# A mixer's attention and recurrence, re-ordered beside a weight stream: rotation next to its projection, ten heads in one staggered sequence, a recurrence without reciprocal

## What is computed

```python
h = rmsnorm(x, g_mix)
q_a, k_a, v_a, x_l, gate_l, q_m, gates = split(h @ w_in)
# local attention: 6 heads of 128, 2 key heads, window of 128 with a sink
q_a, k_a = partial_rope(q_a, positions), partial_rope(k_a, positions)
attn_out = windowed_gqa(q_a, k_a, v_a, attn_sink)
# recurrence in both directions over 768 channels (6 blocks of 128)
xc = centred_depthwise_conv(x_l, conv_w, conv_b)
r, i = sigmoid(xc @ w_r + b_r), sigmoid(xc @ w_i + b_i)
log_a = -8 * r * softplus(-lam)
a = exp(log_a)
bx = sqrt(-expm1(2 * log_a)) * (i * xc)          # then h[t] = a[t] h[t-1] + bx[t]
lru_out = (h_fwd + h_bwd) * gelu(gate_l)
# memory attention: 4 heads over 256 memory rows
mem_out = memory_cross_attention(q_m, k_m, v_m)
g = sigmoid(gates + gate_b)
merged = g0 * (attn_out @ p_attn) + g1 * (lru_out @ p_lru) + g2 * (mem_out @ p_mem)
x = x + merged @ w_out
```

## Time and profile before

| | |
|---|---|
| time, median of 3 runs | 2182.87 us (2181.86 to 2184.75) |
| the profiled execution | 2183.73 us, of which the span takes 2182.0 us |
| the mixer in it | 0 to about 313 us; the part that the change touches, 84 to 240 us |
| PE busy | 2142.5 us, 98% of the span |
| DVE, ACT, POOL busy | 1346.6, 1229.6, 972.0 us |
| granted clock of PE, mean | 0.997 |

### The profile page before, as it was taken

The page is one execution under the profiler, slowest core; times in us unless marked ns, Lnnn a source line. Parts: engine busy times, 40 slices in busy tenths (PEclk is TensorE's granted clock), DMA queues, the critical chain, the costliest instruction groups (busy, mean ns, idle before and its releaser), DMA issues.

```text
span 2182.0 us, 38682 instructions
## 1 busy us (share of the span) xinstructions
PE 2142.5 (98%) x15128; PEld 2009.6 (92%) x15128; DVE 1346.6 (62%) x2631; ACT 1229.6 (56%) x2198; POOL 972.0 (45%) x791
## 2 busy tenths in 40 slices
PE   8999999999999999999999999999999999999999
PEld 7998889999999998888888899899998999899997
DVE  4457652998667756666665865356664864546664
ACT  6567555456777755555555465645445465655443
POOL 5775546999666640000004786560002876561000
PEclk9999999999999999999999999999999999999999
DMA  6443555666444456666665554455665545455665
GB/s 230 153 127 125 161 187 170 187 180 184 143 146 141 144 171 202 193 193 193 193 194 165 184 155 146 136 176 172 184 196 173 176 145 160 133 164 169 186 191 160
DMA packets 102951, 370.16 MB, mean 170 GB/s; under 512 B 11370, under 2 KB 12786, under 8 KB 102132
## 3 DMA queue, kind: packets, MB, share of 16 engines
q1 hardware_dynamic: 102772, 367.69, 54.9%
HBM read 365.53 MB, written 2.11 MB: 168 GB/s over the span
## 4 chain that ended last, share of the span: by engine, by line
PE 85%; DVE 7%; ACT 5%; issue 1%; POOL 1%; DMA 1%; SPq 0%; ACTq 0%; DVEq 0%; POOLq 0%
PE stream_bank L557 16%; PE stream_bank L559 15%; PE stream_bank L558 15%; PE side_bank L557 11%; PE side_bank L558 11%; PE side_bank L559 11%; PE side_bank L856 1%; ACT unit_hi L1124 1%; PE side_bank L855 1%; PE side_bank L635 1%; DVE swa_var L2313 1%; POOL unit_lo L2450 1%; DVE t L1858 1%; PE side_bank L682 1%; ACT squares L1151 1%
## 5 line engine op out<-in xcount | busy, mean ns | idle before, releaser
L2450 POOL TENSOR_TENSOR unit_lo<-raw,unit_hi 128x512 fp32r<-128x512 f32 (+1 forms) x724 | 932.7, 1315 | 404.3 <-ACT unit_hi L1124 403.0
L1124 ACT ACTIVATE unit_hi<-raw 128x1024 fp32r<-128x1024 f32 (+1 forms) x678 | 708.7, 1045 | 195.2 <-PE side_bank L559 73.4
L1676 DVE TENSOR_TENSOR unit_lo<-raw,unit_hi 128x1024 fp32r<-128x1024 f32 (+1 forms) x316 | 389.5, 1233 | 243.1 <-ACT unit_hi L1124 242.5
L557 PE MATMUL stream_bank<-hT_hi,unit_hi 128*128 128x256 f32 x1360 | 400.8, 295 | 4.4 <-POOL unit_lo L2450 4.4
L559 PE MATMUL stream_bank<-hT_hi,unit_lo 128*128 128x256 f32 x1360 | 386.5, 284 | 0.0
L558 PE MATMUL stream_bank<-hT_lo,unit_hi 128*128 128x256 f32 x1360 | 386.4, 284 | 0.0
L557 PE MATMUL stream_bank<-h2T_hi,unit_hi 128*128 128x256 f32 x1152 | 329.6, 286 | 0.0
L559 PE MATMUL stream_bank<-h2T_hi,unit_lo 128*128 128x256 f32 x1152 | 326.0, 283 | 0.0
L558 PE MATMUL stream_bank<-h2T_lo,unit_hi 128*128 128x256 f32 x1152 | 325.8, 283 | 0.0
L557 PEld LDWEIGHTS stream_bank<-hT_hi,unit_hi 128*128 128x128 f32 x1360 | 262.1, 193 | 11.6 <-POOL unit_lo L2450 5.6
L2525 POOL TENSOR_TENSOR gmlp_ws<-gmlp_ws,layer_consts 128x128 f32<-128x128 f32 x8 | 3.4, 461 | 586.5 <-DMA gmlp_ws<-in_gmlp_ws_dram 586.5
(11 more groups left out here) (360 smaller groups left out, 4520.0 us busy)
## 6 DMA issues: line engine op xcount, KB each, us to landing
raw<-in_peer_u_dram SPq DMA_DIRECT2D x128, 512.0 KB, 3.6
raw<-in_peer_v_dram SPq DMA_DIRECT2D x128, 512.0 KB, 3.6
raw<-in_gate_dram SPq DMA_DIRECT2D x64, 512.0 KB, 3.6
raw<-in_gt_dram SPq DMA_DIRECT2D x44, 512.0 KB, 4.2
raw<-in_up_dram SPq DMA_DIRECT2D x44, 512.0 KB, 4.1
raw<-in_ffn_out_dram SPq DMA_DIRECT2D x44, 512.0 KB, 4.2
raw<-in_branch_dram SPq DMA_DIRECT2D x32, 512.0 KB, 3.6
raw<-in_w_gate_dram SPq DMA_DIRECT2D x24, 512.0 KB, 3.6
```

Source lines behind the costliest of these rows:

```text
L557: mm(out, l.hi, r.hi, start=start, stop=False)
L1124: activation(k.unit_hi[n % SPLIT_SLOTS][:, 0:w], k.raw[n % RAW_SLOTS][:, 0:w], ACT.Copy).then_inc(k.sem("unit_hi"), 1)
L1676: V.tensor_tensor(k.unit_lo[s][:, 0:w], k.raw[n % RAW_SLOTS][:, 0:w], k.unit_hi[s][:, 0:w], ALU.subtract).then_inc(unit_lo, 1)
L2450: last = G.tensor_tensor(k.unit_lo[s][:, cols], k.raw[n % RAW_SLOTS][:, cols], k.unit_hi[s][:, cols], ALU.subtract)
```

## The change

`staggered` is `pipeline` with a list of start rounds. The rotation leaves `attention()` and becomes a side generator of its own that starts with unit qk 0, in the order 0 to 7; its matmul goes to side bank `SIDE + 4`, which the recurrence's gates use too, so that these wait for the mark "rope". DVE's product with the sine goes to a scratch tile in SBUF, which frees the bank at once. Memory and local heads form one sequence with the start rounds `HEAD_STARTS`, counted from the round of qm 3. In the recurrence DVE now forms a*a and (a*a + 1) * b, with -0.25 in place of -0.5 under the root. The weights of the recurrence come in six pieces between stream loads. The rest of the diff is semaphore counts for the new order.

```diff
+def staggered(generators, starts):
+    live, rounds = [], 0
+    waiting = list(zip(starts, generators))
+    while waiting or live:
+        while waiting and waiting[0][0] <= rounds:
+            live.append(waiting.pop(0)[1])
...
-ROPE_ORDER = (6, 7, 0, 1, 2, 3, 4, 5)
+HEAD_STARTS = (0, 2, 4, 6, 9, 12, 15, 18, 21, 24)
...
 (PE, lru; the same on ACT and DVE)
+            while "rope" not in at.stages:
+                yield
             for half in range(LRU_BLOCKS // LRU_BATCH):
...
 (PE)
         def rope():
-            for c in ROPE_ORDER:
+            for c in range(8):
                 while not at.reached("qk", c):
                     yield
-                bank = take(SIDE + 2 + ROPE_ORDER.index(c) % 2, ("rope", c))
+                bank = take(SIDE + 4, ("rope", c))
                 pe.wait_ge(*k.over["qk", c])
-                if c == ROPE_ORDER[0]:
+                if c == 0:
                     pe.wait_ge(k.sem("landed_mix_consts"), 16)
+                    pe.wait_ge(k.sem("lru_conv"), LRU_BLOCKS)
                 mm(bank[:, 0:TOKENS], k.swap1, k.qk[:, c, :], start=True, stop=True).then_inc(k.sem("rope_mm"), 1)
                 yield
+            at.stages.add("rope")
             yield
...
-            at.stages.add("p_mem")
-            yield from rope()
-            yield from pipeline([head(Head(k, "attn", h), [k.over["rope", h], k.over["rope", 6 + h // 3], k.over["va", 1]])
-                                 for h in range(Q_HEADS)])
+            attn = [head(Head(k, "attn", h), [(k.sem("rope_done"), 7 + h // 3), k.over["va", 1]]) for h in range(Q_HEADS)]
+            mem[-1] = at.finished("p_mem", mem[-1])
+            yield from staggered(mem + attn, HEAD_STARTS)
             at.stages.add("p_attn")
...
-        at.run(main(), [token_norm(), lru(), attention()])
+        at.run(main(), [token_norm(), lru(), rope(), attention()])
...
 (ACT)
-                activation(b_[:, :, :, :], b_[:, :, :, :], ACT.Sqrt, scale=-0.5).then_inc(k.sem("lru_roots"), 1)
+                activation(b_[:, :, :, :], b_[:, :, :, :], ACT.Sqrt, scale=-0.25).then_inc(k.sem("lru_roots"), 1)
...
 (DVE)
-            own.then(V.tensor_scalar(t1[:, :, :], b_[:, j, :, :], -1.0, 1.0, ALU.mult, ALU.add))
-            own.then(V.reciprocal(t1[:, :, :], t1[:, :, :]))
-            V.tensor_tensor(b_[:, j, :, :], b_[:, j, :, :], t1[:, :, :], ALU.mult)
+            own.then(V.tensor_tensor(t1[:, :, :], a_[:, j, :, :], a_[:, j, :, :], ALU.mult))
+            V.scalar_tensor_tensor(b_[:, j, :, :], t1[:, :, :], 1.0, b_[:, j, :, :], ALU.add, ALU.mult)
...
+                if c >= 2:
+                    dve.wait_ge(k.sem("rope_done"), c - 1)
+                dve.wait_ge(k.sem("rope_mm"), c + 1)
+                V.tensor_tensor(swapped(c), k.bank[SIDE + 4][:, 0:TOKENS], k.rope_s[:, :], ALU.mult).then_inc(
+                    k.free[SIDE + 4], 1)
+                if c:
+                    add(c - 1)
+                yield
...
 (SP)
-    load_until(U["va", 0])
-    fetch(k.lru_w[:, :, :], a["lru_w"].rearrange("p (a e) -> p a e", a=24), "landed_lru_w")
+    for i in range(6):
+        load_until(U["va", 0] + i)
+        fetch(k.lru_w[:, 4 * i:4 * i + 4, :], lru_w[:, 4 * i:4 * i + 4, :], "landed_lru_w")
```

More of the change, by code:

```diff
@@ L249, in pipeline @@
         yield
+def staggered(generators, starts):
+    live, rounds = [], 0
+    waiting = list(zip(starts, generators))
+    assert len(starts) == len(generators)
+    while waiting or live:
+        while waiting and waiting[0][0] <= rounds:
+            live.append(waiting.pop(0)[1])
+        for x in list(live):
+            if next(x, "end") == "end":
+                live.remove(x)
+        rounds += 1
+        yield
 class Own:
@@ L769, in attention @@
                 yield
-            yield from pipeline([head(Head(k, "mem", h), [k.over["qm", h], k.over["km", h], k.over["vm", 1]])
-                                 for h in range(MEM_HEADS)])
-            at.stages.add("p_mem")
-            yield from rope()
-            yield from pipeline([head(Head(k, "attn", h), [k.over["rope", h], k.over["rope", 6 + h // 3], k.over["va", 1]])
-                                 for h in range(Q_HEADS)])
+            mem = [head(Head(k, "mem", h), [k.over["qm", h], k.over["km", h], k.over["vm", 1]]) for h in range(MEM_HEADS)]
+            attn = [head(Head(k, "attn", h), [(k.sem("rope_done"), 7 + h // 3), k.over["va", 1]]) for h in range(Q_HEADS)]
+            mem[-1] = at.finished("p_mem", mem[-1])
+            yield from staggered(mem + attn, HEAD_STARTS)
             at.stages.add("p_attn")
@@ L1298, in attention @@
             act.wait_ge(unit_mm, U["vm", 3] + 1)
-            yield from pipeline([head(Head(k, "mem", h)) for h in range(MEM_HEADS)])
-            at.stages.add("p_mem")
-            yield from rope()
-            yield from pipeline([head(Head(k, "attn", h)) for h in range(Q_HEADS)])
+            mem = [head(Head(k, "mem", h)) for h in range(MEM_HEADS)]
+            mem[-1] = at.finished("p_mem", mem[-1])
+            yield from staggered(mem + [head(Head(k, "attn", h)) for h in range(Q_HEADS)], HEAD_STARTS)
             at.stages.add("p_attn")
@@ L1913, in rope, with add @@
         def rope():
-            turned = lambda i: k.bank[SIDE + 2 + i % 2][:, 0:TOKENS]
-            def add(i):
-                c = ROPE_ORDER[i]
-                dve.wait_ge(k.sem("rope_mul"), i + 1)
-                V.tensor_tensor(k.qk[:, c, :], k.qk[:, c, :], turned(i), ALU.add).then_inc(k.free[SIDE + 2 + i % 2], 1)
-            for i, c in enumerate(ROPE_ORDER):
+            swapped = lambda c: k.squares[:, 0, c % 2 * TOKENS:(c % 2 + 1) * TOKENS]
+            def add(c):
+                dve.wait_ge(k.sem("rope_mul"), c + 1)
+                dve.wait_ge(*k.over["rope", c])
+                V.tensor_tensor(k.qk[:, c, :], k.qk[:, c, :], swapped(c), ALU.add).then_inc(k.sem("rope_done"), 1)
+            for c in range(8):
                 while not at.reached("qk", c):
                     yield
-                if i == 0:
+                if c == 0:
                     dve.wait_ge(k.sem("rope_tables"), 1)
-                dve.wait_ge(k.sem("rope_mm"), i + 1)
-                own.then(V.tensor_tensor(turned(i), turned(i), k.rope_s[:, :], ALU.mult))
-                if i:
-                    add(i - 1)
+                if c >= 2:
[5 more added lines that the diff above has]
+                    add(c - 1)
                 yield
-            add(len(ROPE_ORDER) - 1)
+            add(7)
+            at.stages.add("rope")
             yield
@@ L2474, in rope @@
         def rope():
-            yield from steps(4)
-            while not at.reached("qm", MEM_HEADS - 1):
-                yield
-            yield from pipeline([steps(6) for h in range(MEM_HEADS)])
-            for i, c in enumerate(ROPE_ORDER):
+            for c in range(8):
                 while not at.reached("qk", c):
                     yield
-                if i == 0:
+                if c == 0:
                     pool.wait_ge(k.sem("rope_tables"), 1)
-                pool.wait_ge(k.sem("rope_mm"), i + 1)
+                pool.wait_ge(k.sem("rope_mm"), c + 1)
                 G.tensor_tensor(k.qk[:, c, :], k.qk[:, c, :], k.rope_c[:, :], ALU.mult).then_inc(k.sem("rope_mul"), 1)
```

14 lines of the change are left out of this document (10 added, 4 removed).

## The result

The changed kernel takes 2190.06 us (median of 7 runs, 2187.04 to 2196.93) against 2183.83 us for the kernel before on the same chip (7 runs, 2180.07 to 2185.03): a ratio of 1.0032, 95% interval 1.0023 to 1.0041. It is slower, by 5 to 9 us. The profiled execution took 2189.36 us, of it 2188.0 us of span.

The account below looks back on a forecast made before the run. PE, busy 98% of the span, bounds the kernel; 17.5 us of lost PE time could be won. Rotation 5.0, head waits 9.2 and slow clock 0.8 make 15.0 lost: -2.5 us, 2180.4 us, own range 2177 to 2184, whole range 2173 to 2187.5.

Parts of the forecast that it names:

- Rotation, +5.0: Rounds 21 to 28: PE waits for ACT's eviction of the unit just ended, 0.63 us per rotation, eight times.
- Memory heads without waits, old rotation wait gone: Three memory-head waits beside the recurrence go (-2.8 -0.5 us), and the old rotation's wait too (-1.5 -0.16).
- Recurrence's operations: New pair on DVE takes 2.34 us instead of 4.52, gaining 2.2 per block, 13 in all; PE's waits unaltered.
- Table loads: Rounds 29 to 34: gelu alternating with exp adds six ACT table loads of 1.28 us, 7.7 us; 14 in the stretch.
- D: Rival: a table switch costs twice its load because ACT empties first; +7.7 us, 2188.1 us; chance 0.04.
- Rounds 31 to 37, 5.0: PE waits for late ACT at local heads' transposes and V products: 0.9, 0.95, 1.7, 0.6 and 0.8 us.
- Round 39, 2.0, at most 3.4: A local head's normalisation waits for DVE, which scans behind the late square root: 0.8 to 3.4 us, 2.0 taken.
- Pipelining: Pipelining lost at each wait, 0.16 us, said to be included in the 9.2 us of new waits at local heads.
- Behind that nothing: After round 48 no PE waits: stream data is split three units ahead, ACT never over two rounds late.
- C: Slower rival: rounds 21 to 28 chain PE to ACT, each rotation wait 1.9 us; +10.2, 2190.6 us; chance 0.10.
- B: Faster rival: local heads' waits vanish, only 2 of 9.2 us stay; -9.7, 2173.2 us; chance 0.22.
- E: Rival: heads' waits stay at today's size, from ACT's own queue, and eviction waits are added; 2186.2 us; chance 0.14.

Follow-up runs that it names:

- e4: Kernel before with only the recurrence's part of the change (no reciprocal; product and fused multiply-add instead): 2181.71 us, 0.9992 of before.
- e5: Changed kernel with the recurrence's gates back beside the rotation, in rounds 21 to 26 as before the change: 2183.3 us, 0.9995 of before.
- e6: e5 with the rotation one round behind its unit and local heads starting in rounds 33 to 53, 4 apart: 2181.39 us, 0.9987 of before.
- e11: e5 with the rotation one round behind its unit and local heads from the second on one round later: 2180.45 us, 0.9984 of before.
- e12: e6 with only the local heads' starts changed, to rounds 32, 35, 39, 42, 46 and 49: 2175.8 us, 0.9965 of before.
- e8: Changed kernel with side steps inside a round reordered on ACT and DVE, heads first, recurrence last: 2190.63 us, 1.0033 of before.
- e13: e12 with the last local head starting in round 52 instead of 49: 2175.02 us, 0.9966 of before.
- e1: Changed kernel with the rotation one round behind its unit and local heads from the second on one round later: 2189.44 us, 1.0032 of before.
- e9: e6 with side steps inside a round reordered on ACT and DVE, heads first, recurrence last: 2183.02 us, 0.999 of before.
- e10: e4 with side steps inside a round reordered on ACT and DVE, heads first, recurrence last: 2185.8 us, 1.0007 of before.
- e14: e12 with the 1 MB load of the residual input issued behind all loads of the branch projections: 2173.68 us, 0.9955 of before.
- e16: e13 with the residual input's load issued behind those of the branch projections: 2175.0 us, 0.9963 of before.
- e2: Changed kernel with the low half of stream unit 41 made by POOL instead of DVE: 2191.9 us, 1.0044 of before.

## Why the prediction was wrong

Forecast -2.5 us, range 2173 to 2187.5; measured 2190.06, +6.2 us. In the order of its working:

- **Rotation, +5.0.** The mechanism is right, the size a little small: eight waits of 0.52 to 0.62 us, 4.5 idle and 8 x 0.23 lost around them, some 6.3. No wait of PE in rounds 21 to 30 is for DVE's or POOL's steps of the rotation.
- **Memory heads without waits, old rotation wait gone.** Right; there is none in rounds 24 to 30. The reason given, the recurrence beside them, is not shown: e4, without the reciprocal, keeps 2.2 us of the 2.8, and e5, with the recurrence back beside them, has none; e6, e11 and e12 have 0.7. What e5, e6, e11, e12 and after share, and e4 lacks, is the rotation in these rounds; it was not tested by itself.
- **Recurrence's operations.** The pair takes 0.74 + 1.18 = 1.92 us, not 2.34: DVE gains 2.6 us a block and 0.5 of the affine step by the medians, and 18.5 us in the sum over the six blocks. Its total falls by 13.8 only, among other things because the rotation's add, which now reads both operands from SBUF, takes 6.8 us instead of 3.4. As said, it moves PE little.
- **Table loads.** Fourteen in the stretch, as forecast, 1.28 us each, the next activation 0.01 to 0.02 us behind. D falls: the Trainium skill, "ScalarE: Activation LUTs", section "What ACT_TABLE_LOAD costs", adds a drain to each load, and these loads show none behind them (nor a gap above 0.02 us ahead).
- **Rounds 31 to 37, 5.0.** Measured 0.91, 1.10, 1.64, 0.63, 0.71: 5.0. Laying out ACT's steps from the earlier trace rows was good to 0.15 us for each wait.
- **Round 39, 2.0, at most 3.4.** The first step that failed: 5.03 us. ACT was laid out step by step, DVE only as "scans behind the late square root". What was left out is that ACT's split of the first scanned block, DVE's `lo` and second scan, the inverse and ACT's normalisation wait for each other in turn. e8 shows that it was this order (0.81 us without it).
- **Round 48, 2.2.** Measured 1.69.
- **Half a clock slowdown, 0.8.** Measured 6.8 us at half clock, some 2.0 lost. It came with the long wait, so this error of 1.2 us hangs on the one above.
- **Pipelining** of the heads' seven waits was said to be in the 9.2, which adds up idle times alone. Measured 0.7 for the three V products and 0.8 for the four transposes: 1.5 us.
- **"Behind that nothing".** The second step that failed: 3.4 us idle in seven gaps of rounds 59 to 78 and 0.25 lost at each, 5.2 us in all. I looked for whether the branches were ready and whether the stream was three units ahead, and not at what the recurrence, now ending beside short rounds, does to ACT's splits and so to the loads.

Lost in 84 to 240 us: forecast 15.0, measured 16.2 idle, 3.3 at 15 gaps and 2.0 at half clock, 21.5. The kernel before lost 14.0 + 2.2 + 1.7 = 17.9 there in the same count, not 17.5. So up to the first matmul of a branch output the sum is +3.6, and the traces have +3.8 (162.3 us from the first score before, 166.1 after); from there to the stretch's end they have +5.2, which is the second failed step. Behind the stretch this profile is 3.1 us shorter than that of before. One period less at half clock is up to 1.7 of it; the rest is open.

Much of it hangs on one omission: the recurrence's move by nine rounds had no term of its own. I followed the heads and the rotation, and gave the recurrence a date by which it had to end. e5 undoes that move alone and takes back 6.8 us, as much as was lost against before, though not the same microseconds: the 5.0 of rounds 31 to 37, which the sum had, go with it, and the late waits stay. Those go only where the heads end later as well (e6, and in part e13). None of the signs that the prediction named could warn: the eight rotation waits, the fourteen loads, the waits of rounds 31 to 37 and the quiet memory heads all came true. They test the terms that had a price, and not those put at nothing. The rivals: C's figure, 2190.6, is nearly the one measured, but its mechanism is not there (no eviction wait above 0.62 us). B fell by the heads' waits; E's figure lies in between, but its claim that the old waits stay does not hold for the memory heads. That C's figure was met is luck.

## What to carry to other kernels

When side work is moved along a stream, price each generator that moves with it, also the one that only makes room, and lay out every engine whose queue its steps share, to the end of the last one. Where two engines are late together, a taken-away wait or another order in the queue shows up elsewhere (e1, e8, e9, e10); what helped is to keep small operations that PE needs out of the rounds in which a long one stands in front of them (e12). The fastest kernel here by its median, e14, keeps the early recurrence, lets the rotation lag a round, starts the heads clear of the scans and loads the residual late: 0.9955 of before, interval 0.9941 to 0.9969. The intervals of e12, e13 and e16 overlap with it, so the last step's gain in time is not shown.

## What the runs showed of the hardware

A product of 128x2 numbers on DVE took 1.15 us beside a split on POOL and 0.13 without one; a scan 1.66 and 0.69. A tiny operation can so cost as much as a large one. The Trainium skill, "SBUF — State Buffer", section "Who interferes with whom", calls the port pair that DVE and GpSimd share an exclusive lock; the trace of e2 agrees, as the small product ended with POOL's split, at 173.56.

Of the eight waits of PE above 4 us in the stretches of these profiles six lie with 6.83 us at half clock and two with 3.41; of the kernels whose longest wait in the stretch is 2.66 us or less, five have none there and three (before, e4, e11) 3.41 us. What such a period costs depends on what PE does in it: 0.21 instead of 0.12 us from one matmul of the stream to the next, and nothing where it waits anyway.
